# Hybrid S5 and retention layer on one core: the first four tiles of x in a new order, and fillers of zeros on TensorE

## The reference, cut to what matters

```python
def rmsnorm(x, g):
    x32 = x.astype(jnp.float32)
    y = x32 * lax.rsqrt(jnp.mean(x32 * x32, axis=-1, keepdims=True) + EPS)
    return (y * g.astype(jnp.float32)).astype(x.dtype)

z = rmsnorm(h, norm_mix[l])
proj = z @ w_in[l]
u, q, k, v, g, gate_a, gate_b = jnp.split(proj, IN_SPLITS, axis=-1)
...
h = h + merged @ w_out[l]
z = rmsnorm(h, norm_mlp[l])
h = h + jnp.square(jax.nn.relu(z @ w_up[l])) @ w_down[l]
return rmsnorm(h, norm_final)
```

## Time and profile before

| | |
|---|---|
| median of 3 runs | 1557.47 us (1557.12 to 1557.95) |
| profiled execution, its own time | 1558.99 us |
| its span, first to last instruction | 1557.2 us |
| mean granted TensorE clock | 0.994 of full speed |
| TensorE (PE) busy | 1513.8 us, 97% |
| VectorE (DVE) busy | 949.6 us, 61% |
| GpSimd (POOL) busy | 434.9 us, 28% |
| ScalarE (ACT) busy | 301.5 us, 19% |

### The profile page before, as it was taken

How to read it: one execution, slowest core, us unless ns; L and a number is a source line. 1 busy time by engine, 2 the same in 40 slices (tenths; PEclk the granted TensorE clock), 3 DMA queues, 4 the chain that set the end, 5 groups by cost and what they waited for, 6 DMA issues and landing times.

```text
span 1557.2 us, 21285 instructions
## 1 busy us (share of the span) xinstructions
PE 1513.8 (97%) x7474; PEld 1266.0 (81%) x7474; DVE 949.6 (61%) x1925; ACT 301.5 (19%) x580; POOL 434.9 (28%) x363
## 2 busy tenths in 40 slices
PE   5999999999999999999999999999999999999996
PEld 4888888789898988878888777888888888888885
DVE  7896756553565646466625688555555555555557
ACT  4211111310222222231101322111111111101114
POOL 5010102221010100003333003444444444444444
PEclk9999999999999999999999999999999999999998
DMA  7124434364110110103542010111111111111113
GB/s 225 68 95 108 142 104 106 106 213 149 32 55 27 44 37 27 55 27 122 175 170 68 1 41 14 55 54 54 54 54 54 54 52 43 54 54 54 43 43 131
DMA packets 98565, 119.18 MB, mean 77 GB/s; under 512 B 16296, under 2 KB 66640, under 8 KB 98512
## 3 DMA queue, kind: packets, MB, share of 16 engines
q1 hardware_dynamic: 67520, 78.22, 15.9%
q10 hardware_dynamic: 30992, 40.26, 8.2%
HBM read 96.56 MB, written 20.97 MB: 75 GB/s over the span
## 4 chain that ended last, share of the span: by engine, by line
PE 86%; DVE 9%; ACT 2%; ACTq 1%; issue 1%; DMA 0%; DVEq 0%; SPq 0%
PE acc L643 21%; PE acc L645 21%; PE acc L644 21%; PE aux L643 6%; PE aux L645 6%; PE aux L644 6%; DVE h_res L2127 1%; PE aux L902 1%; PE aux L896 1%; PE aux L905 1%; ACTq L1178 1%; DVE s_lo L2113 1%; PE aux L795 1%; DVE y_raw L1839 1%; PE aux L789 1%
## 5 line engine op out<-in xcount | busy, mean ns | idle before, releaser
L2127 DVE TENSOR_TENSOR h_res<-h_res,acc 128x512 f32<-128x512 f32 x240 | 159.9, 685 | 98.0 <-PE acc L645 97.3
L643 PE MATMUL acc<-dw_hi,hid_hi 128*128 128x512 f32 x512 | 199.6, 390 | 1.0 <-DVE h_res L2127 1.0
L644 PE MATMUL acc<-dw_lo,hid_hi 128*128 128x512 f32 x512 | 199.4, 389 | 0.0
L645 PE MATMUL acc<-dw_hi,hid_lo 128*128 128x512 f32 x512 | 199.4, 389 | 0.0
L517 POOL CAST w_hi<-stage 128x1024 fp32r<-128x1024 f32 x44 | 50.9, 1173 | 495.9 <-PE acc L645 333.7
L643 PE MATMUL acc<-w_hi,z_hi 128*128 128x256 f32 (+1 forms) x512 | 189.0, 369 | 0.0
L643 PE MATMUL acc<-z_hi,w_hi 128*128 128x512 f32 x448 | 178.4, 398 | 6.1 <-DVE z_lo L1499 5.9
L644 PE MATMUL acc<-z_lo,w_hi 128*128 128x512 f32 x448 | 176.0, 393 | 0.0
L645 PE MATMUL acc<-z_hi,w_lo 128*128 128x512 f32 x448 | 175.7, 392 | 0.0
L645 PE MATMUL acc<-w_hi,z_lo 128*128 128x256 f32 (+1 forms) x512 | 173.0, 338 | 0.0
L644 PE MATMUL acc<-w_lo,z_hi 128*128 128x256 f32 (+1 forms) x512 | 172.8, 338 | 0.0
(11 more groups left out here) (327 smaller groups left out, 2932.6 us busy)
## 6 DMA issues: line engine op xcount, KB each, us to landing
stage<-in_w_up SPq DMA_DIRECT2D x32, 512.0 KB, 4.0
stage<-in_w_down SPq DMA_DIRECT2D x32, 512.0 KB, 3.3
stage<-in_w_in SPq DMA_DIRECT2D x28, 512.0 KB, 4.1
gate_dram<-gate_t ACTq DMA_DIRECT2D x32, 256.0 KB, 2.1
x_in<-in_x SPq DMA_DIRECT2D x8, 512.0 KB, 7.0
stage<-in_w_in SPq DMA_DIRECT2D x32, 128.0 KB, 2.8
stage<-in_w_in SPq DMA_DIRECT2D x16, 256.0 KB, 3.2
gb_t<-gate_dram ACTq DMA_DIRECT2D x16, 256.0 KB, 2.8
```

The lines of the kernel that those rows point to most:

```text
L643: nc.tensor.matmul(out, s_hi, m_hi_, start=first, stop=False)
L644: nc.tensor.matmul(out, s_hi, m_lo_, start=False, stop=False)
L645: return nc.tensor.matmul(out, s_lo, m_hi_, start=False, stop=last)
L2127: V.tensor_tensor(h_res[:, c, hs], h_res[:, c, hs], acc[:, p % 4, :], ALU.add)\
```

## The change

- SyncE: the step sizes and the parameter rows go behind x tiles 1 to 3, the identity and the first weight load; the second weight load goes behind tile 4.
- GpSimd first writes zeros into a new bf16 tile `warm` of 128x128.
- TensorE multiplies `warm` by itself: 44 times before tile 0, 12 times between tiles 0 and 1, 16 times between tiles 1 and 2. The parameter transposes go behind tile 3 and into `aux`, behind `lo_done` 4. Tiles 2 and 3 go into the four banks of `acc` in place of `aux`.
- ScalarE first waits for the identity. It makes the scaled identities itself (four of them, `diag` has four places). Its order becomes: squares 0 and 1, identity 0, squares 2 and 3, identity 1, `hi_z(0)`, `hi_z(1)`, identities 2 and 3, `hi_z(2)`, `hi_z(3)`, the parameter copies, squares 4 to 7, `hi_z(4)` and on.
- VectorE makes root 0, root 1, roots 2 and 3 side by side, `lo_z(0)` and `lo_z(1)`, the spread copy, `lo_z(2)` and `lo_z(3)`, and roots 4 to 7 side by side from 128x1 operations.

```diff
@@ sync
             sp.dma_start(nmix[:], ...).then_inc(const_in, 16)
+            sp.dma_start(x_in[:, 1, :], x_rows[:, 1, :]).then_inc(x_ready[1], 16)
+            sp.dma_start(ident[:], t["ident"]).then_inc(ident_in, 16)
+            for c in range(2, 4):
+                sp.dma_start(x_in[:, c, :], x_rows[:, c, :]).then_inc(x_ready[c], 16)
+            load(0, w_in[:, 0:2, 0:HALF])
             sp.dma_start(ls_raw[...], t["log_step"]...).then_inc(ls_in, 16)
-            sp.dma_start(x_in[:, 1, :], x_rows[:, 1, :]).then_inc(x_ready[1], 16)
-            sp.dma_start(ident[:], t["ident"]).then_inc(ident_in, 16)
...
-            for c in range(2, NCH):
+            sp.dma_start(x_in[:, 4, :], x_rows[:, 4, :]).then_inc(x_ready[4], 16)
+            load(1, w_in[:, 2:4, 0:HALF])
+            for c in range(5, NCH):
                 sp.dma_start(x_in[:, c, :], x_rows[:, c, :]).then_inc(x_ready[c], 16)
-                if c in (3, 4):
-                    load(c - 3, ...)
@@ gpsimd
+            nc.gpsimd.memset(warm[:], 0.0).then_inc(warm_in, 1)
             pool.wait_ge(const_in, 16)
@@ tensor
-                    if n >= 4:
+                    if n >= 8:
                         pe.wait_ge(lo_done, SP_Z + n - 3)
+                    if n == 11:
+                        pe.wait_ge(prm_ready, 1)
+                    bank = acc if c in (2, 3) else aux
...
+            def warm_up(n):
+                for _ in range(n):
+                    nc.tensor.matmul(acc[:, 3, 0:P], warm[:], warm[:], start=True, stop=True)
+            pe.wait_ge(warm_in, 1)
+            warm_up(44)
             pe.wait_ge(ident_in, 16)
             turn_x(0)
+            warm_up(12)
+            turn_x(1)
+            warm_up(16)
+            turn_x(2)
+            turn_x(3)
             pe.wait_ge(lam_in, 16 * 4)
             pe.wait_ge(ls_wide, 1)
+            pe.wait_ge(lo_done, SP_Z + 4)
...
-            for c in range(1, 4):
-                turn_x(c)
             pe.wait_ge(lo_done, SP_Z + 8)
-            pe.wait_ge(prm_ready, 1)
@@ scalar
+            def diag_x(c):
+                act.wait_ge(x_rooted, c + 1)
+                nc.scalar.activation(diag[:, c, :], ident[:], ACT.Copy, scale=rs1[:, c:c + 1]).then_inc(diag_ready, 1)
+            act.wait_ge(ident_in, 16)
+            square_x(0)
+            square_x(1)
+            diag_x(0)
+            square_x(2)
+            square_x(3)
+            diag_x(1)
+            hi_z(0)
+            hi_z(1)
+            diag_x(2)
+            diag_x(3)
+            hi_z(2)
+            hi_z(3)
+            act.wait_ge(prm_turned, 1)
...
+            for c in range(4, NCH):
                 square_x(c)
@@ vector
+            def root_rows(p, n, told):
+                dve.wait_ge(ss_done, p + n)
+                ...
+                for i in rows:
+                    ins = V.tensor_scalar(m[i], a[i], -0.5 / D, -0.5 * EPS, ALU.mult, ALU.add)
+                link(ins)
+                ...
+                for step in range(3):
+                    for i in rows:
+                        ins = V.tensor_scalar(y2[i], y[i], y[i], m[i], ALU.mult, ALU.mult)
+                    link(ins)
+                    for i in rows:
+                        ins = V.tensor_scalar(r[i] if step == 2 else y[i], y2[i], 1.5, y[i], ALU.add, ALU.mult)
+                ...
+            root_x(0)
+            dve.wait_ge(x_rooted, 1)
+            root_x(1)
+            dve.wait_ge(x_rooted, 2)
+            root_rows(2, 2, True)
+            for c in range(4):
+                lo_z(c)
+                if c == 1:
+                    dve.wait_ge(ls_in, 16)
+                    V.tensor_copy(prm[STATE:STATE + PAIRS, :]...).then_inc(ls_wide, 1)
             dve.wait_ge(const_in, 16)
-            rstd_x(4, 4)
+            root_rows(4, 4, False)
             for c in range(4, NCH):
                 norm_x(c)
```

More of the change, by code:

```diff
@@ L199, in build @@
             ls_raw = sb("ls_raw", [P, 16], F32, r)
-            diag = sb("diag", [P, 2, P], F32, r)
-            sb("x_pad", [P, 736], F32, r)
+            diag = sb("diag", [P, 4, P], F32, r)
+            warm = sb("warm", [P, P], BF16, r)
+            sb("x_pad", [P, 416], F32, r)
             coef = sb("coef", [P, 56, PAIRS], F32, r)
@@ L303, in build @@
         x_scaled = sem("x_scaled")
+        x_rooted = sem("x_rooted")
+        warm_in = sem("warm_in")
         x_weighted = sem("x_weighted")
@@ L690, in turn_x @@
                     n = 2 * c + b
-                    if n >= 4:
+                    if n >= 8:
                         pe.wait_ge(lo_done, SP_Z + n - 3)
+                    if n == 11:
+                        pe.wait_ge(prm_ready, 1)
+                    bank = acc if c in (2, 3) else aux
                     for q in range(4):
                         k = 4 * b + q
-                        out, x = aux[:, n % 4, q * P:(q + 1) * P], x_in[:, c, k * P:(k + 1) * P]
+                        out, x = bank[:, n % 4, q * P:(q + 1) * P], x_in[:, c, k * P:(k + 1) * P]
                         if c < 4:
-                            mm = nc.tensor.matmul(out, x, diag[:, c % 2, :], start=True, stop=True)
+                            mm = nc.tensor.matmul(out, x, diag[:, c, :], start=True, stop=True)
                         else:
@@ L1095, in hi_z @@
                     act.wait_ge(z_turned, n + 1)
+                    bank = acc if c in (2, 3) else aux
                     hi_split(z_hi[:, 4 * b:4 * b + 4, c * P:(c + 1) * P],
-                             aux[:, n % 4, :].rearrange("p (k s) -> p k s", k=4))
-            for c in range(4):
-                square_x(c)
[L1101 to L1112, removed]
+                             bank[:, n % 4, :].rearrange("p (k s) -> p k s", k=4))
+            def diag_x(c):
[15 more added lines that the diff above has]
+            act.wait_ge(prm_turned, 1)
+            nc.scalar.activation(coef[:, 0:2, :], aux[:, 3, 0:2 * PAIRS].rearrange("p (i q) -> p i q", i=2), ACT.Copy)
+            nc.scalar.activation(skip_glu[:], aux[:, 3, 2 * PAIRS:40].rearrange("p (i m) -> p i m", i=2), ACT.Copy)
+            nc.scalar.activation(coef[:, 2, :], aux[:, 3, 40:40 + PAIRS], ACT.Copy).then_inc(prm_ready, 1)
+            for c in range(4, NCH):
+                square_x(c)
+            for c in range(4, NCH):
                 hi_z(c)
@@ L1544, in lo_z @@
                     dve.wait_ge(hi_done, SP_Z + n + 1)
+                    bank = acc if c in (2, 3) else aux
                     lo_split(z_lo[:, 4 * b:4 * b + 4, c * P:(c + 1) * P],
[L1546 removed]
+                             bank[:, n % 4, :].rearrange("p (k s) -> p k s", k=4),
                              z_hi[:, 4 * b:4 * b + 4, c * P:(c + 1) * P])
[L1549 to L1551 removed]
@@ L1552, in diag_x, with root_x @@
[L1552 to L1566, removed]
+            def root_x(c):
+                dve.wait_ge(ss_done, c + 1)
+                rstd(rs1[:, c:c + 1], ss1[:, c:c + 1], D, x_rooted)
@@ new lines, in root_rows @@
+            def root_rows(p, n, told):
+                dve.wait_ge(ss_done, p + n)
+                rows = range(n)
+                m, y, y2 = [[rs_tmp[:, k, i:i + 1] for i in rows] for k in range(3)]
+                bits, a, r = [[x[:, o + i:o + i + 1] for i in rows] for x, o in ((rs_bits, 0), (ss1, p), (rs1, p))]
+                for i in rows:
+                    ins = V.tensor_scalar(m[i], a[i], -0.5 / D, -0.5 * EPS, ALU.mult, ALU.add)
+                link(ins)
+                for i in rows:
+                    ins = V.tensor_scalar(bits[i], m[i].bitcast(I32), 1, None, ALU.arith_shift_right)
+                link(ins)
+                for i in rows:
+                    ins = V.tensor_scalar(y[i].bitcast(I32), bits[i], -1.0, ROOT_BITS, ALU.mult, ALU.add)
+                link(ins)
+                for step in range(3):
+                    for i in rows:
+                        ins = V.tensor_scalar(y2[i], y[i], y[i], m[i], ALU.mult, ALU.mult)
+                    link(ins)
+                    for i in rows:
+                        ins = V.tensor_scalar(r[i] if step == 2 else y[i], y2[i], 1.5, y[i], ALU.add, ALU.mult)
+                        if step == 2 and told:
+                            ins.then_inc(x_rooted, 1)
+                    if step < 2 or not told:
+                        link(ins)
```

11 lines of the change are left out of this document (5 added, 6 removed).

## The result

The changed kernel takes 1564.53 us (median of 6 runs, 1562.86 to 1566.85) against 1557.30 for the kernel before on the same chip: **ratio 1.0043, 95% interval 1.0033 to 1.0052**. The profiled execution took 1564.13 us, its span is 1562.3, 5.1 us more than that of before. I had forecast 1559.0 and "no change", with an upper end of 1561.2. That was wrong.

A forecast was written before the change was run, and what follows sets the result against it. TensorE, 97% busy, bounds the kernel; only its list's start, at tile 4, can move. Root 4.2 us later, 2.7 shorter, norm the same: +1.5 on 1557.47 gives 1559.0; range 1555.9 to 1561.2.

The forecast's parts named there:

- Which view bounds the kernel, and tile 4: First 40 us: TensorE bounds and waits last for tile 4's norm; tile 4 at 36.45 against 34.88, +1.5 us.
- Before tile 0: Identity lands 5.1 us after issue, first square at 7.2, root 0 starts where it did, tile 0 at 11.2.
- The fillers' time: On TensorE, 44 fillers last 4.4 to 7.5 us; the 28 between tiles take 0.1 each, 2.8 us.
- Clock down in tile 0: TensorE idles 2.6 to 5.7 us before tile 0, its clock falls again, and tile 0 takes 3.76 us.
- rival 5: At the start, zeros do not raise TensorE's clock at all; changes little, at most the 28 fillers' low-clock cost; no chance given.
- rival 1: TensorE's clock stays up through tile 0: -0.2 us, 1557.3; chance 0.25.
- Rival 2: The 28 fillers between the tiles are slower, at the low clock: +3.5 us, 1561.0; chance 0.12.
- rival 4: TensorE's clock holds over the last gap, before tile 4: -1.7 us, down to 1555.6; chance 0.09.
- Squares and roots: Squares 4 to 7 run from 24.7 to 29.6; their four roots take 5.5 us against 8.16, ending at 35.1.
- Rival 3: VectorE's roots of tiles 4 to 7 are held by GpSimd, one to 33.3: +4.7 us, 1562.2; chance 0.04.
- Behind it: After tile 4: clock falls as before, 1.7 us for 1.7; VectorE's coefficient chain and all later loads move with it.

The follow-up runs named there:

- the repeat: The changed kernel run once more, unedited: 1564.97 us, ratio 1.0040.
- the 88: The changed kernel with 88 fillers ahead of tile 0 in place of 44, the 12 and 16 kept: 1559.74 us, ratio 1.0006.
- the repaired start: The changed kernel, 72 fillers kept, with squares 4 and 5 earlier and roots 4 to 7 as two pairs, each followed by its norms: 1559.52 us, 1.0008.
- before + 44: The kernel before with only the 44 fillers ahead of tile 0 added: 1556.20 us, ratio 0.9988.

## Why the prediction was wrong, step by step

**Which view bounds the kernel, and tile 4.** Held. TensorE waited last for `norm_x(4)`. Forecast for tile 4: 36.45, +1.5. Measured 35.86 and 36.23 in two traces with fillers, 36.23 without. Taken alone, this part is right in the total also: the kernel without fillers is at 1.0005, +0.8 us (-0.5 to +2.2), against my +1.5.

**Before tile 0.** The identity landed 5.92 us behind its issue, not 5.1; the first square started at 8.07, not 7.2, and this time it was the last to arrive. Root 0 at 9.25 and tile 0 at 12.04, each 0.8 later than I had them.

**The fillers' time.** 44 in 4.83 us, which is 0.110 each and inside my bounds (4.4 to 7.5); 12 in 0.99 (1.37 in the repeat), 16 in 1.06, less in this trace than the 0.1 each that I took. The second 44 of the 88 took 2.5 us (7.36 less 4.83), 0.057 each. Both levels are thus near my lower bounds, the 128 columns alone (0.107 and 0.053); the first 44 ran nearly all at the low one. The Trainium skill (TensorE: Matmul & The Clock Gate, Back-to-back issue gap) has about 81 ns for such a warm pair; by that, as an estimate, the 28 would take 2.3 us. The rows give 2.05 for the two groups.

**Clock down in tile 0.** Held: 3.75 us for the tile, granted clock 0.50, after 6.20 idle us. The fillers raised the clock (12 products a us, then 22, in the trace with 88) and it was gone when it was wanted. That excludes rival 5, and rival 1 did not come either; with 88 fillers and 3.63 idle us the tile still took 3.17. Rival 2 is excluded by 2.05 us for the 28. The fall before tile 4 came too, and the low stretch lasted to about 39.8: rival 4 excluded.

**Squares and roots.** Forecast: squares from 24.7 to 29.6, roots 5.5 us long to 35.1. Measured 24.02 to 28.9, 5.5 to 34.5. The timeline of VectorE has the operations in groups of four, beside GpSimd's splits:

```profile
29.02 0.33 DVE L1583 TENSOR_SCALAR rs_tmp<-ss 128x1 f32<-128x1 f32 x4 [4.34 <-ACT x_junk L1106]
...
33.06 0.82 DVE L1593 TENSOR_SCALAR rs_tmp<-rs_tmp 128x1 f32<-128x1 f32 x4
```

Rival 3 (roots held by GpSimd) did not happen: one-column operations with one tensor input ran at the speed of rows 11 beside a split. The Trainium skill (GPSIMD Engine Reference, Specifications; VectorE: DVE Perf Modes, Mode 2×_2P) has one-source float32 operations among those that contend with GpSimd; at 128x1, 0.15 to 0.27 us each, none in this trace shows it. Rows 4 show the 128x4 operation with two tensor inputs that does wait.

**The step that failed** is "Behind it": "VectorE's coefficient chain and all later loads move with tile 4", with its premise in the first paragraph, that TensorE "has a list without long gaps, so the change can only move the point at which that list starts". TensorE's products move with tile 4, though not one for one: 7.3 us gained at tile 4 with the repaired start were 3.3 by 60 us. Its instruction fetches don't move with it: they are set by the count of instructions, and the change adds 144. I had costed a filler as time on the array alone and found it hidden; as an instruction it was not hidden, it was only charged 250 and 1500 us later. The sum lacked that term: 5.7 us between with and without fillers, 1.0036 for the same 144 instructions in the kernel before. In the trace of the profiled execution it is 2.7 at 275 us and 1.7 at 1532. The row that would have warned me is in the page of before, queue q8, 33 packets of 16 KB, 0.2% of DMA time; the prediction does not use it.

**The range** held rival 1 to 2 and single falls of the clock. It had no case in which something off the first 40 us changed, so 1564.5 lay 3.3 us above its end, and "slower by over 0.2%" with 0.12 was too low. The base of the sum took 1.5 us of the profiled execution for profiling. That did not repeat: the changed kernel's profiled execution is 0.4 us below its median. The first trace's fall of the clock at 971, 1.6 us, is as large.

What stays open: why the seven issues lengthen by 0.4 in one kernel and by 1.0 in another. In each of them one issue alone is long, the seventh in the changed kernel's first trace (1.02 us for 0.62), the sixth in the others (1.10 to 1.67), and the fetch lies 3.0 to 3.6 us behind the first issue. And why the gain of "before + 44" is there, as said above.

## What to carry to other kernels

An added instruction has two costs, its time on the engine and its place in the engine's instruction stream. In a kernel with chains of small, latency-bound transfers, look in the DMA view for the `instruction` queue, and see before and after an edit whether a fetch falls into such a transfer; a test is to add or take some cheap instructions in an idle wait and leave all else alone. A difference of 0.4% between two versions may be nothing but that, and so compare two ideas at more than one count of instructions. Warming an engine ahead of a gap is only worth what is left of it when the work comes: here 44 and 88 products of zeros had raised the clock, and it was down again in tile 0.

## What the runs showed of the hardware that I had not expected

- TensorE's instructions come in packets of 16384 bytes, each taking 0.88 to 1.86 us, about one for 256 weight loads and matmuls, and none in the later passes of a loop. A load of 512 KB that met one took 5.0 to 5.5 us; without one 3.3 to 3.7.
- Delay grows on its way. 0.4 us in ScalarE's queue became 1.1 us of waiting on TensorE through VectorE's collision with GpSimd, and 2.7 with the clock; 1.0 us became 3.9 of waiting (5.47 against 1.53).
- The same kernel's start differs from execution to execution: tile 4 of the kernel before at 34.88 in one trace and 36.45 in the next.
